# State-space scan of an encoder layer: tables first, inputs before lag products, scan in place in two PSUM banks

## What is computed

```python
dt = jnp.exp(log_dt)[:, None];  mag = jnp.exp(lam_re * dt)
ar, ai = mag * jnp.cos(lam_im * dt), mag * jnp.sin(lam_im * dt)
bu_re = jnp.einsum('blgc,gpc->blgp', u, bb_re)      # and bu_im
s_re, s_im = scan(s = a * s_prev + bu, reverse=reverse)   # complex, along the 512 tokens
y = einsum('blgp,gcp->blgc', s_re, c_re) - einsum('blgp,gcp->blgc', s_im, c_im)
```

## Time and profile before

| | |
|---|---|
| median of 3 runs | 2135.89 us (2134.34 to 2136.89) |
| the profiled execution | 2133.08 us, its span 2131.0 us |
| TensorE matmul, busy | 1787.5 us, 84% |
| VectorE, busy | 1433.7 us, 67% |
| GpSimd, busy | 1119.2 us, 53% |
| ScalarE, busy | 567.0 us, 27% |
| mean granted clock of TensorE | 0.946 of 2.4 GHz |
| state-space blocks, from latents(0) to the end of `Y(3)` | 65.7 to 214.4 us |

### The profile page before, as it was taken

The page is one execution under the profiler, slowest core; times in us unless marked ns, Lnnn a source line. Parts: engine busy times, 40 slices in busy tenths (PEclk is TensorE's granted clock), DMA queues, the critical chain, the costliest instruction groups (busy, mean ns, idle before and its releaser), DMA issues.

```text
span 2131.0 us, 19420 instructions
## 1 busy us (share of the span) xinstructions
PE 1787.5 (84%) x5959; PEld 974.9 (46%) x5959; DVE 1433.7 (67%) x2983; ACT 567.0 (27%) x1271; POOL 1119.2 (53%) x1171
## 2 busy tenths in 40 slices
PE   5878799999999969978789689878868877887687
PEld 5546434778996754433333233323323333332233
DVE  6598774444443488777777786677677777777763
ACT  3334443222333231213112311221122112312211
POOL 6990000000000066777777677767767767777772
PEclk9998899999999989999999989989999999999899
DMA  4311401334342089999999999999999999999995
GB/s 121 66 14 20 109 1 36 103 90 153 99 136 92 1 312 399 406 409 408 407 409 409 406 409 409 406 409 409 406 404 409 406 388 410 409 396 409 409 409 216
DMA packets 239391, 603.06 MB, mean 283 GB/s; under 512 B 38533, under 2 KB 105274, under 8 KB 239290
## 3 DMA queue, kind: packets, MB, share of 16 engines
q0 software_dynamic: 147840, 537.99, 63.9%
q1 hardware_dynamic: 91450, 63.85, 10.8%
HBM read 597.56 MB, written 2.10 MB: 281 GB/s over the span
## 4 chain that ended last, share of the span: by engine, by line
PE 26%; DMA 25%; DVE 25%; issue 14%; POOL 6%; ACT 2%; SPq 1%; DVEq 0%; ACTq 0%; POOLq 0%
PE bank L1587 19%; DMA slabs<-in_peer_u,R 8%; DMA WS<-in_peer_u,R 7%; DMA R<-in_peer_u,R 6%; PE bank L1899 5%; DVE R L1474 3%; DVE R L1014 2%; DMA R<-in_peer_v,R 2%; POOL R L2026 2%; PE bank L1879 2%; DVE R L1427 2%; DVE R L1430 2%; DVE H L1488 2%; DVE R L1428 1%; DVE R L1426 1%
## 5 line engine op out<-in xcount | busy, mean ns | idle before, releaser
L1899 PE MATMUL bank<-R 128*128 128x512 f32 x2048 | 977.5, 628 | 230.2 <-ACT R L947 154.0
L1899 PEld LDWEIGHTS bank<-R 128*128 128x128 f32 x2048 | 392.7, 199 | 804.0 <-issue 606.2
L2026 POOL DMA_INDIRECT R<-in_peer_v,R x512 | 491.7, 960 | 164.6 <-issue 136.0
L2026 POOL DMA_INDIRECT WS<-in_peer_u,R x172 | 165.1, 960 | 650.7 <-DVEq L1461 586.8
L1474 DVE CUSTOM_DVE_ANT_0 R<-WS,bank 128x1024 f32<-128x1024 f32 x172 | 210.0, 1221 | 97.0 <-issue 83.9
L1474 DVE CUSTOM_DVE_ANT_0 R<-slabs,bank 128x1024 f32<-128x1024 f32 x168 | 205.1, 1221 | 101.8 <-issue 90.7
L1474 DVE CUSTOM_DVE_ANT_0 R<-R,bank 128x1024 f32<-128x1024 f32 x172 | 210.0, 1221 | 89.6 <-issue 77.9
L1587 PE MATMUL bank<-R 128*64 128x64 f32 (+6 forms) x792 | 193.3, 393 | 36.5 <-ACT R L714 12.7
L940 ACT ACTIVATE R<-R 128x16 f32<-128x16 f32 x32 | 6.9, 216 | 779.0 <-DVE R L1474 779.0
L2026 POOL DMA_INDIRECT slabs<-in_peer_u,R x168 | 161.9, 964 | 82.1 <-issue 36.6
L2026 POOL DMA_INDIRECT R<-in_peer_u,R x172 | 165.6, 963 | 62.9 <-issue 36.9
(11 more groups left out here) (216 smaller groups left out, 1951.1 us busy)
## 6 DMA issues: line engine op xcount, KB each, us to landing
slabs<-in_w_in SPq DMA_DIRECT2D x17, 512.0 KB, 5.3
slabs<-in_w_mem_kv SPq DMA_DIRECT2D x8, 1024.0 KB, 5.5
slabs<-in_w_peer_q SPq DMA_DIRECT2D x8, 1024.0 KB, 16.8
R<-in_peer_v,R POOLq DMA_INDIRECT x512, 17.9
slabs<-in_w_in SPq DMA_DIRECT2D x4, 1024.0 KB, 14.2
slabs<-in_w_ssm_glu SPq DMA_DIRECT2D x16, 256.0 KB, 3.1
slabs<-in_w_out SPq DMA_DIRECT2D x4, 1024.0 KB, 5.2
slabs<-in_w_mem_q SPq DMA_DIRECT2D x4, 1024.0 KB, 5.2
```

What stands on the lines that cost most here:

```text
L1899: last = pe.matmul(ps[2 * (t % 2) + n][:, :], diag[s % DRING], Vb[i % VRING][:, 512 * n:512 * n + 512], start=(s == 0), stop=(s == TOPK - 1))
L2026: pool.indirect_dma_start(out=dst, out_offset=None, in_=table, in_offset=bass.IndirectOffsetOnAxis(ap=ix[:, s:s + 1], axis=0)).then_inc(si ...
```

## The change

GpSimd runs all six table levels first and `output_matrices(0)` behind them; VectorE waits for the table only at its first scan stage, behind `contributions(1)`. On TensorE the chunk inputs of a block go in front of its lag products (`turned`, `lagged` and `inputs` replace `prep`), and blocks overlap in another order. In the scan stage `X` stays in its two banks: products, sums and scans write back into banks 6 and 7, half of the products to `t4` in SBUF, and `Z`, `Zs` go; the two banks are drained only when `Sst` is written. During the scan the banks are given out by kind: `X` has 6 and 7, `Y` always 5, all other jobs 0 to 4 in turn. ScalarE's queue follows the new order, with `gelu(0)` and `gelu(1)` behind the squares.

```diff
+    j += latents(0) + turned(0) + inputs(0) + latents(1) + turned(1) + lagged(0) + inputs(1)
+    j += latents(2) + [("Y", 0)] + turned(2) + lagged(1) + inputs(2)
+    j += [("Y", 1)] + lagged(2) + turned(3) + lagged(3) + inputs(3)
+    j += [("Y", 2), ("kvn",), ("qn",), ("Y", 3)]
...
-            b = i % 8 if i < tail else (i - tail) % 6
+            if scan[0] <= i <= scan[1]:
+                if k[0] == "X":
+                    b = 6 + k[2]
+                elif k[0] == "Y":
+                    b = 5
+                else:
+                    b = turn_of % 5
+                    turn_of += 1
...
+            latents(0)
+            inputs_prep(0)
+            act.wait_ge(zeros_set, 1)
+            decays(0)
             windows(0)
+            latents(1)
+            inputs_prep(1)
+            lags_out(0)
+            decays(1)
+            latents(2)
+            windows(1)
+            inputs_prep(2)
+            lags_out(1)
+            decays(2)
+            windows(2)
+            lags_out(2)
+            inputs_prep(3)
+            windows(3)
+            decays(3)
+            lags_out(3)
...
-                tt(t4[0], xr[:, :], tc, ALU.mult)
-                tt(t4[2], xr[:, :], ts, ALU.mult)
-                dve.sem_inc(empty(("X", q, 0)), 1)
-                tt(t4[1], xi[:, :], ts, ALU.mult)
-                tt(t4[3], xi[:, :], tc, ALU.mult)
-                dve.sem_inc(empty(("X", q, 1)), 1)
-                tt(Z[0], t4[0], t4[1], ALU.add)
-                tt(Z[1], t4[3], t4[2], ALU.subtract)
+                if q == 0:
+                    dve.wait_ge(table_done, 1)
+                xr = await_full(dve, ("X", q, 0))[:, :]
+                xi = await_full(dve, ("X", q, 1))[:, :]
+                tt(t4[0], xr, tc, ALU.mult)
+                tt(xr, xr, ts, ALU.mult)
+                tt(t4[1], xi, tc, ALU.mult)
+                tt(xi, xi, ts, ALU.mult)
+                tt(xi, t4[0], xi, ALU.add)
+                tt(xr, t4[1], xr, ALU.subtract)
...
+                step(dve.tensor_tensor_scan(xi, m8, xi, 0.0, ALU.mult, ALU.add))
+                signal(dve.tensor_tensor_scan(xr, m8, xr, 0.0, ALU.mult, ALU.add), scanned, q + 1)
+                tt(t4[0], xi, tc, ALU.mult)
+                tt(t4[1], xr, tc, ALU.mult)
+                tt(xr, xr, ts, ALU.mult)
+                tt(xi, xi, ts, ALU.mult)
...
                 dve.wait_ge(s_done, 4 * (q + 1))
+                for r in range(2):
+                    dve.sem_inc(empty(("X", q, r)), 1)
...
+            latents(0)
+            turned(0)
...
+            chunk_inputs(0)
+            latents(1)
+            turned(1)
+            lagged(0)
+            chunk_inputs(1)
+            latents(2)
+            block_outputs(0)
+            turned(2)
+            lagged(1)
+            chunk_inputs(2)
+            block_outputs(1)
+            lagged(2)
+            turned(3)
+            lagged(3)
+            chunk_inputs(3)
+            block_outputs(2)
...
-            for n in range(5):
+            for n in range(6):
                 table_level(n)
+            pool.sem_inc(table_done, 1)
             pool.wait_ge(pow_done, 1)
-            output_matrices(0)
-            table_level(5)
-            pool.sem_inc(table_done, 1)
-            for q in range(1, NB):
+            for q in range(NB):
                 output_matrices(q)
```

More of the change, by code:

```diff
@@ L111, in latents, with turned, lagged, inputs @@
         return [key for key, _, _ in LATENT_JOBS[2 * n:2 * n + 2]]
[L113 to L122, removed]
+    def turned(b):
+        return [("bT", b, r, s) for r in range(2) for s in range(2)]
+    def lagged(b):
+        return [("D", b, s) for s in range(NB)]
+    def inputs(b):
+        return [("X", b, 0), ("X", b, 1)]
+    j += latents(0) + turned(0) + inputs(0) + latents(1) + turned(1) + lagged(0) + inputs(1)
+    j += latents(2) + [("Y", 0)] + turned(2) + lagged(1) + inputs(2)
+    j += [("Y", 1)] + lagged(2) + turned(3) + lagged(3) + inputs(3)
+    j += [("Y", 2), ("kvn",), ("qn",), ("Y", 3)]
     j += [("yt", q) for q in range(G // 4)] + [("yT", f) for f in range(4)]
@@ L388, in encoder_layer @@
         tail = jobs.index(("mo", 0, 0))
-        place, uses = {}, [0] * 8
+        scan = (jobs.index(LATENT_JOBS[0][0]), jobs.index(("Y", NB - 1)))
+        place, uses, turn_of = {}, [0] * 8, 0
         for i, k in enumerate(jobs):
-            b = i % 8 if i < tail else (i - tail) % 6
+            if scan[0] <= i <= scan[1]:
[6 more added lines that the diff above has]
+                    turn_of += 1
+            else:
+                b = i % 8 if i < tail else (i - tail) % 6
             place[k] = (b, uses[b])
@@ L715, in windows, with inputs_prep @@
                                    w[64:128, :, 1:, :].rearrange("p g j c -> p g (j c)"), ACT.Copy).then_inc(ext_done, 1)
-            def block_prep(q):
+            def inputs_prep(q):
                 if q:
@@ L723, in block_prep, with lags_out @@
                         copy_out(("bT", q, r, s), BT[r][:, 4 * s:4 * s + 4, :].rearrange("p g n -> p (g n)"), b[:, :])
+            def lags_out(q):
                 if q:
@@ L743, in gelu, with latents @@
                 act.activation(yq, yq, ACT.Gelu_apprx_tanh).then_inc(yg_done, 1)
-            for key, _, _ in LATENT_JOBS[0:2]:
-                latent(key)
-            windows(0)
[L748 to L767, removed]
+            def latents(n):
+                for key, _, _ in LATENT_JOBS[2 * n:2 * n + 2]:
+                    latent(key)
+            latents(0)
+            inputs_prep(0)
+            act.wait_ge(zeros_set, 1)
+            decays(0)
+            windows(0)
+            latents(1)
[13 more added lines that the diff above has]
+            lags_out(3)
+            for m in range(3):
+                act.activation(latsq[:, m, :], cqT[:, m, :], ACT.Square).then_inc(lat_sq, 1)
+            for m in range(2):
+                act.activation(latsq[:, 3 + m, :], ckvT[:, m, :], ACT.Square).then_inc(lat_sq, 1)
+            gelu(0)
+            gelu(1)
+            for k in range(2):
+                act.wait_ge(lat_var, k + 1)
+                act.activation(lat[k], lat[k], ACT.Sqrt).then_inc(lat_std, 1)
+            gelu(2)
             gelu(NB - 1)
@@ L1630, in latent, with turned @@
                 product(key, lambda b: [(b[:, :], [(w[:, k, at:at + 128], FT[:, k, :]) for k in range(KD)])])
-            def block_prep(q):
+            def turned(q):
                 pe.wait_ge(vb_done, 2 * (q + 1))
@@ L1638, in block_prep, with lagged @@
                             for g in range(4)])
+            def lagged(q):
                 pe.wait_ge(ext_done, 6 * (q + 1))
@@ L1654, in chunk_inputs, with latents, block_outputs @@
                         for lo, way in ((0, 1), (64, -1)) for g in range(GB)])
[L1656 to L1673, removed]
+            def latents(n):
+                for entry in LATENT_JOBS[2 * n:2 * n + 2]:
+                    latent(*entry)
+            def block_outputs(q):
                 pe.wait_ge(d_within, 16 * CH * (q + 1))
@@ L1680, in _ @@
                                              (wim[:, g, :], Sst[1][:, g, :])]) for g in range(GB)])
+            latents(0)
+            turned(0)
+            for q in range(G // 4):
+                await_drained(pe, ("uT", q))
+            chunk_inputs(0)
[14 more added lines that the diff above has]
+            block_outputs(2)
+            pe.wait_ge(lat_sq, 5)
+            pe.wait_ge(ones_set, 1)
+            product(("kvn",), lambda b: [(b[:, :], [(ones[:, :], latsq[:, 3 + m, :]) for m in range(2)])])
+            product(("qn",), lambda b: [(b[:, :], [(ones[:, :], latsq[:, m, :]) for m in range(3)])])
+            block_outputs(3)
             pe.wait_ge(yg_done, NB)
```

13 lines of the change are left out of this document (1 added, 12 removed).

## The result

The changed kernel takes 2141.48 us (median of 20 runs, 2138.38 to 2146.05), beside 2135.78 for the kernel before (20 runs, 2133.02 to 2141.69): +5.7 us, ratio 1.0027, 95% interval 1.0021 to 1.0033. It is slower by a little, as forecast (2141.0). The profiled execution has a span of 2138.7 us, against 2131.0.

What follows compares the result with a forecast made beforehand. VectorE and TensorE, both near full, wait for each other in turn, and the last `Y` sets the end; `Y(3)` ending 5.0 us later, added to the median 2135.9, gave 2141 us (chance 0.60), own range 2138 to 2144.5.

Steps and rivals of the forecast that it cites:

- Scan stage beside GpSimd 12.8 us: VectorE's scan stage in PSUM: 12.8 us at any time, saving 9.4 us in block 0, about 7 in block 1.
- rival 2: VectorE's eight PSUM writes of stage 3 are slow: up to 6.4 us more, 2147 us; chance 0.07.
- rival 3: PSUM operand does not free GpSimd, stages 0 and 1 stay at 22 and 20 us: 2142.5; chance 0.05.
- Tables at 78.8: GpSimd's last table level, started at 61.6, ends at 78.8 us, 15.8 us earlier than before.
- `Y(1)` 5.0 us idle, then wholly slow, 10.2: TensorE idles 5.0 us for block 1's lag DMAs; clock falls, `Y(1)` runs 150.6 to 160.8.
- Rival 1: `Y(1)` keeps the full clock: -5.1 us there, -2.2 in `D(2)`, time 2133.6; chance 0.22.
- Rival 4: Both gaps shrink as DMAs land or GpSimd finishes block 0 earlier: below 2131.6 us; chance 0.06.
- `D(3)` 4.8 us behind the windows: Before `D(3)`, TensorE idles 4.8 us for ScalarE's `windows(3)`, queued behind the turns' copies, done at 176.2.
- `Y(3)` behind `outputs(2)`, 8.1 us behind the last sums: `Y(3)` waits for shared bank 5, drained by VectorE's `outputs(2)` 8.1 us after stage 3: starts 209.2, not 204.8.
- End of `Y(3)` at 219.4, +5.0: After 11 us idle `Y(3)` runs 10.2 us at the lower clock, ending at 219.4 against 214.4.
- what moves the end of `Y(3)`, 214.4, moves the whole, one for one: Rotary-stage DMAs start when `Y(3)` is full, so a shift of its end shifts the whole time equally.
- `output_matrices(0)`, foreseen at 20.2 us: GpSimd's first output matrices run 78.8 to 99.0: 15.0 alone, plus 5.1 for six instructions meeting VectorE.

Runs made afterwards that it cites:

- experiment 2: Changed kernel with five extra 128x512 products into bank 5 in the idle place before `Y(1)`; 2138.28 us, ratio 1.0008.
- Experiment 1: Changed kernel with `outputs(2)` on VectorE moved ahead of the variances and scaled latents of the last block; 2135.7 us, ratio 0.9996.
- experiment 8: Changed kernel with `outputs(2)` ahead of variances and scaled latents, five extra products before `Y(1)` and five before `Y(3)`; 2134.62 us, ratio 0.9988.
- experiment 6: Changed kernel with `windows(3)` ahead of `inputs_prep(3)` on ScalarE; 2139.74 us, ratio 1.0021.
- experiments 4: Kernel before with only the tables made ahead of `output_matrices(0)` and VectorE's wait for them behind `contributions(1)`; 2137.82 us, ratio 1.0006.
- experiment 5: Changed kernel without the scan in place, products, scans and states through `Z` and `Zs` as before; 2144.07 us, ratio 1.0047.
- experiment 9: Kernel before with four extra 128x512 products into `Y(3)`'s own bank between the norm products and `Y(3)`; 2135.13 us, ratio 0.9997.
- the last run of experiment 10: Kernel before with scan in place, `X` in banks 6 and 7, the rest over 0 to 5, four extra products before `Y(3)`; 2132.14 us, ratio 0.9981.
- experiment 3: Kernel before with only the scan stage in place in PSUM, old order, banks and tables; 2130.42 us, ratio 0.9966.

## Why the prediction was right, step by step

**The forecast stood, with its mechanism.** Six of its steps against the trace:

- *Scan stage beside GpSimd 12.8 us:* 12.6 (95.12 to 107.7). A product that writes PSUM takes 0.70 us, one that only reads it 0.69: rival 2 is out, and rival 3 by the same rows. The 0.8 us a block that the prediction estimated from the errata table (the Trainium skill's page VectorE: DVE Perf Modes) are not seen: the stage took 12.6 us, against 12.8 in the kernel before.
- *Tables at 78.8:* GpSimd passes to the output matrices at 78.36 (below); it began the level at 61.62, as foreseen.
- *`Y(1)` 5.0 us idle, then wholly slow, 10.2:* 5.29 and 10.4. Rival 1, a kept clock, did not come of itself; made by hand (experiment 2) it was worth some 7 us at `Y(3)` and 4.7 in the time. So the place where the prediction saw its decision was a right one. Rival 4, shorter gaps, did not come either.
- *`D(3)` 4.8 us behind the windows:* 5.19.
- *`Y(3)` behind `outputs(2)`, 8.1 us behind the last sums:* 212.64 - 204.19 = 8.45. Idle for 11.36 us, foreseen 11. Experiment 1 took 6.6 us off and gave back 7.3.
- *End of `Y(3)` at 219.4, +5.0:* 223.1 in this trace, +8.7 against the profile before. The two profiled executions are 7.6 us apart, the medians 5.7.

**What was mis-sized.** The sum is 3.7 us short at the end of `Y(3)`, and 2.4 of them are there when `X(1)` ends, at 117.1 instead of 114.7. Two terms are behind that. The first is `output_matrices(0)`, foreseen at 20.2 us with six of its twelve instructions meeting VectorE. It took 21.6 (78.36 to 99.93), and eight met VectorE, since VectorE was late: the prediction took it that the last table level costs VectorE nothing, but the level lies beside `contributions(0)`, with 128x1024 operands on both sides:

```profile
64.17 6.11 DVE L1038 TENSOR_TENSOR R<-R 128x1024 f32<-128x1024 f32 x2
```

```profile
65.99 3.21 POOL L1982 TENSOR_TENSOR XN<-WS 128x1024 f32<-128x1024 f32 x1
...
78.36 1.86 POOL L1982 TENSOR_TENSOR H<-R 128x512 f32<-128x512 f32 x1 [0.18 <-POOL R L1982]
```

Two VectorE products take 6.11 us beside these, against 4.21 beside 128x512 ones (88.83, above). `contributions(0)` took 17.1 us instead of 12.6 and, also begun 3.7 us later than in the kernel before, ended at 81.3 instead of 73.0. The 0.5 us that the turns at 81.36 waited for it were not on the path: TensorE came to the last four turns early and waited for ScalarE there. But `D(0)` began at 105.6 instead of 104.8. How long the turns wait for VectorE differs from one execution to the next: not at all in experiment 8, 2.30 us in experiment 6, with the same program up to there.

The second term is larger: `D(0)` with `X(1)`, sized at 9.9 us, took 11.58, since after 1.96 us of idleness ahead of the last four transposes the clock fell. No step of the prediction had a fall there, and it was not bound to come: in experiments 2 and 6 it did not. The last 1.3 us are small excesses behind that, of the lag DMAs, `D(3)` with `X(3)`, the drain and `Y(3)`.

**A step that did not hold in general** is "what moves the end of `Y(3)`, 214.4, moves the whole, one for one". Against the profile before, the changed kernel has +8.7 us at `Y(3)` and +7.7 in the span; experiments 4, 5 and 6 have +3.1, +10.0 and +4.9 at `Y(3)` and +3.3, +10.9 and +6.2 in the span. There it holds within 1.3 us. But where extra products had kept the clock up through `Y(3)`, 3.7 to 5.0 us were lost behind it: experiment 9 has -1.8 at `Y(3)` and +3.2 in the span, experiment 8 -0.6 and +3.1, the last run of experiment 10 -5.8 and -0.9. Each of these is one execution, beside a profile of before that is 2.7 us under its own median.

So the nearness of 5.7 to the forecast of 5.0 is in part luck: the sum was 3.7 us short at `Y(3)`, and of the 8.7 us of this trace only 5.7 are left in the medians.

**Where did the gain go?** The scan in place wins 7 us alone (experiment 3). The order with the tables first loses 8 to 10 (experiment 5). Together they are +5.7, where addition would give +1 to +3: in the new order the scan in place is worth only 2 to 4 us of the time, and 0.3 at `Y(3)`; the rest of what VectorE gains is spent waiting, since TensorE stands for DMAs, windows and bank 5.

## What to carry to other kernels

Before reordering around an engine that is nearly 90% busy (VectorE's 106.2 of 120 us), take away its cost first and look at what is late then: here the in-place scan alone was worth more than it with the reordering. When a buffer is given to one kind of result for good, find who drains it and what stands ahead of that in its engine's order; moving two instructions (`outputs(2)`) won back about the whole loss. Fill an idle gap of TensorE only where nothing else ends within the same few us, and with products that don't wait for what the gap waits for.

## What the runs showed of the hardware

- With one operand in PSUM, VectorE was as fast as with all in SBUF, and GpSimd did not slow it: 0.69 to 0.70 us for a 128x512 product either way. A scan in place in a bank took 1.23 us beside busy GpSimd, one from SBUF to SBUF 2.01 (experiment 5), and 1.23 when GpSimd was done.
- Ahead of the last four turns before `D(0)` TensorE was idle 1.96 us in the changed kernel (then 11.58 us for the 96 products of `D(0)` and `X(1)`), 1.93 in experiment 1 (11.60), 3.68 in experiment 8 (12.15), 0.78 in experiment 2 (9.99) and not at all in experiment 6 (9.99). The length of the gap alone doesn't decide: in the kernel before, the clock stayed at 1.00 through 2.23 us of idleness that ended at 186.34.
- Once it had fallen, the clock stayed at 0.50 through all of `Y(1)` and `Y(3)`, 10.4 us each, and came back in `D(2)` behind `Y(1)`, begun at 163.80: 0.53 at 165 to 167 us, 1.00 at 167 to 169.
- Keeping the clock up in one place moved its fall to the next: at 1.00 through `Y(3)` in experiment 9, 0.50 at 216 us.
